# Attention tail sums spread one to every three steps, and a reordered start of the first unit

## Chip, core and metric

The kernel runs on one core of a Trainium2 chip. Its engines are PE (TensorE, matrix products and transposes), ACT (ScalarE), DVE (VectorE), POOL (GpSimd) and SP, whose queue issues the DMAs. Each engine runs its own instructions strictly in the order in which the program holds them, and waits for semaphores of the others. The metric is the device time of one execution in microseconds (us); lower is better.

## What is computed

The reference is three blocks in a row on a sequence of 1024 tokens and width 1024: a hybrid layer (stick-breaking attention and two gated linear recurrences), a block of an RWKV time mix beside a dilated window attention, and a block of spatial gating and Fourier mixing. The change touches two places: the very first projection, and the dilated attention, for each of 16 heads of width 64:

```python
DILATED_PATTERNS = ((128, 1), (512, 4), (2048, 16))

def mixed_dilated_attention(p_att, gate):
    q, k, v = (t.reshape(B, S, ATT_HEADS, HEAD_DIM) for t in jnp.split(p_att, 3, axis=-1))
    for window, dilation in DILATED_PATTERNS:
        o, lse = dilated_window_attention(q, k, v, window, dilation)   # softmax inside a window
        ...
    wts = jax.nn.softmax(jnp.stack(lses, axis=0), axis=0)
    o = jnp.sum(wts[..., None] * jnp.stack(outs, axis=0), axis=0)
    return o.reshape(B, S, ATT_W) * jax.nn.silu(gate)
```

## The kernel before

**The first unit.** A "unit" is one 128-column slice of a projection: its weights W (128 x 1024 f32) are loaded, split by ACT into a rounded part (`w_hi`) and by DVE into the rest (`w_lo`), and PE multiplies with the input, which is split in the same way into `xs` (`x_hi` on ACT, `x_lo` on DVE), in eight slices k. Each of the two halves of 512 tokens takes 8 x 3 matmuls of 128x512 (`mm3`), so a unit is 48 matmuls. At the start SP issues the eight slices of the input first, and then the weights of the first two units (`b1_sp`). ACT and DVE split all eight slices and do five tiny operations on gate constants (`lbl`, with one exponential `lb_exp` on ACT) before the split of the first weights (`b1_act`, `b1_dve`). `unit_pe` does half 0 through all eight slices and then half 1. After four units the stick-breaking attention begins (`sb_act`, `sb_dve`).

**The dilated attention** runs over eight pairs of heads, p = 0 to 7. What each engine does for a pair is written as generators that yield at each step, and `weave` takes one step of each in turn, which fixes the order of an engine's instructions: in a stage p the main part of pair p (39 steps), the tail of pair p-1, and the three projection units of pair p+1 (8 steps each, so they fill steps 0 to 23). Steps are counted from 0 here.

- Main (`att_pe_main`, `att_act_main`, `att_dve_main`): ten pieces. In step 3i PE makes the scores of piece i, DVE adds the mask and takes the minimum (`a_max`), ACT takes the exponential (`a_exp`); in step 3i+1 PE turns (transposes) the exponentials of piece i-2 (`a_t`, two PSUM banks, one for each head) and DVE copies them out (`PT`); in step 3i+2 PE multiplies piece i-3 with the values (`a_av`), and ACT copies finished outputs (`a_osc`).
- Tail: POOL spreads the minima (x = 0) and the sums (x = 1) of the softmax over a tile `XM`, six copies each; PE turns each with four transposes (`spread_pe`, `xm_t`). ACT copies those of x = 0 to `MB`, DVE forms the common minimum and the differences (`mb_min`, `mb_sub`), ACT their exponentials (`mb_e`), DVE weights and adds the three outputs (`o_w`, `o_add`), multiplies by the gate (`gated_o`), multiplies the turned sums of x = 1 into `MB` (`den`), adds them (`den_sum`), takes the reciprocal in four pieces and multiplies it in (`att_out`), which SP stores.
- The turned exponentials and the turned `XM` take the same two PSUM banks in turn (ring `RT`). An `a_t` that falls on the bank of an `xm_t` of x = 1 waits for its `den`.
- The third unit of a stage is the gate. Its eviction on ACT (a silu, line L301, in steps 21 and 23) writes the buffer that `gated_o` of the pair two before reads, which is the pair whose tail runs in the same stage; so it waits for that `gated_o` (`att_units_act`).

After the last pair its tail runs alone; then follows the next part of the kernel, whose constants are loaded after the store of the last `att_out`.

## Time and profile before

| | us |
|---|---|
| median of 3 runs | 3436.62 |
| lowest and highest | 3430.69, 3438.08 |
| the profiled execution | 3428.97 |
| its span | 3427.6 |
| the six attention stages with a tail and units | 82.1 to 84.1 each |

The profiled execution is one run; the views below are all read from it. Each stage of the attention is measured from the start of one pair's first scores (or its last transposes) to the same point of the next.

### The profile page before, as it was taken

The page shows a single profiled execution, that of the slowest core. Times are in us where ns is not written, and L with a number is a line of the kernel's source. Part 1 is how long each engine was busy: PE and PEld are TensorE (multiplying, and loading weights), DVE is VectorE, ACT ScalarE, POOL GpSimd, SP SyncE. Part 2 cuts the span into 40 slices and gives each one's busy share as a digit, 9 for nine tenths or more (in the row PEclk, how much of TensorE's full clock was granted, in tenths as well). Part 3 has the DMA queues.
Part 4 walks back from the last instruction along what each step waited for, and adds up shares of the span by engine and source line. Part 5 has one row for each costly group of instructions (what it writes and reads, how often), then busy time and mean ns, then how long its engine had stood idle before and what let it go on. Part 6 is the DMA issues. An engine that isn't in the chain of part 4 may idle for free. (4 is left out here: it accounts for less than half of the span.)

```text
span 3427.6 us, 66797 instructions
## 1 busy us (share of the span) xinstructions
PE 3070.9 (90%) x28304; PEld 2464.4 (72%) x28304; DVE 1946.3 (57%) x3481; ACT 1326.7 (39%) x2364; POOL 127.4 (4%) x132
## 2 busy tenths in 40 slices
PE   7988999999989988888867999969898889999998
PEld 5665777866767766666645787859787887777876
DVE  3555566523474367677764545646666666545465
ACT  3344343221244455555551444422222223453224
POOL 0000000000000112112210000000000000000000
PEclk9998999999999999999988999979999999999999
DMA  3000011242245311111101233341112115341114
GB/s 109 19 19 19 31 39 55 62 165 70 75 133 166 94 40 48 44 45 49 44 32 50 80 129 129 117 189 50 50 55 73 47 56 210 123 140 62 37 46 157
DMA packets 106089, 270.73 MB, mean 79 GB/s; under 512 B 8880, under 2 KB 49472, under 8 KB 104256
## 3 DMA queue, kind: packets, MB, share of 16 engines
q1 hardware_dynamic: 105792, 266.47, 23.3%
q8 instruction: 224, 3.67, 0.5%
q14 instruction: 73, 0.60, 0.1%
HBM read 209.81 MB, written 56.62 MB: 78 GB/s over the span
## 5 line engine op out<-in xcount | busy, mean ns | idle before, releaser
L197 PE MATMUL ps<-xs,wparts 128*128 128x512 f32 (+1 forms) x1664 | 697.2, 419 | 29.2 <-DVE wparts L265 28.3
L199 PE MATMUL ps<-xs,wparts 128*128 128x512 f32 (+1 forms) x1664 | 656.5, 395 | 0.0
L198 PE MATMUL ps<-xs,wparts 128*128 128x512 f32 (+1 forms) x1664 | 655.8, 394 | 0.0
L265 DVE TENSOR_TENSOR wparts<-wring,wparts 128x1024 fp32r<-128x1024 f32 x248 | 305.8, 1233 | 327.4 <-ACT wparts L257 301.5
L197 PEld LDWEIGHTS ps<-xs,wparts 128*128 128x128 f32 (+1 forms) x1664 | 315.5, 190 | 131.5 <-issue 59.9
L257 ACT ACTIVATE wparts<-wring 128x1024 fp32r<-128x1024 f32 x248 | 262.8, 1060 | 299.2 <-PE ps L199 210.8
L199 PEld LDWEIGHTS ps<-xs,wparts 128*128 128x128 f32 (+1 forms) x1664 | 314.5, 189 | 71.9 <-issue 0.6
L198 PEld LDWEIGHTS ps<-xs,wparts 128*128 128x128 f32 (+1 forms) x1664 | 316.0, 190 | 60.8 <-issue 4.6
L2066 ACT ACTIVATE Pm<-Pm,ml 128x128 f32<-128x128 f32 (+1 forms) x384 | 167.4, 438 | 178.0 <-DVE ml L2131 177.8
L2131 DVE CUSTOM_DVE_ANT_0 Pm<-ps,mask 128x128 f32<-128x128 f32 (+1 forms) x384 | 110.4, 347 | 139.0 <-PE ps L1974 139.0
L2427 ACT ACTIVATE M<-ps 128x256 f32<-128x256 f32 x160 | 61.5, 384 | 255.7 <-PE ps L2238 246.9
L2523 DVE COPY_PREDICATED XX<-lm,ps 128x512 f32<-128x512 uint8 (+1 forms) x160 | 107.9, 674 | 79.8 <-PE ps L2238 76.7
L2238 PE MATMUL ps<-XX,M 64*64 64x64 f32 x2560 | 144.4, 219 | 5.7 <-issue 3.1
L1987 PE MATMUL ps<-cc,Pm 128*128 128x128 f32 x560 | 83.6, 289 | 67.1 <-DVE MB L2179 50.1
L197 PE MATMUL ps<-wparts,mixA 128*128 128x512 f32 x320 | 129.0, 403 | 12.2 <-DVE wparts L265 9.4
L2238 PEld LDWEIGHTS ps<-XX,M 64*64 64x64 f32 x2560 | 128.9, 135 | 9.3 <-issue 6.5
L2238 PE MATMUL ps<-M,XX 64*64 64x64 f32 x2048 | 124.9, 218 | 2.5 <-issue 2.5
L1987 PEld LDWEIGHTS ps<-cc,Pm 128*128 128x128 f32 x560 | 66.4, 147 | 83.2 <-DVE MB L2179 52.7
L199 PE MATMUL ps<-wparts,mixA 128*128 128x512 f32 x320 | 126.0, 394 | 0.0
L198 PE MATMUL ps<-wparts,mixA 128*128 128x512 f32 x320 | 125.7, 393 | 0.0
L197 PE MATMUL ps<-wparts,xs 128*128 128x512 f32 x256 | 105.0, 410 | 13.7 <-DVE wparts L265 13.7
L2238 PEld LDWEIGHTS ps<-M,XX 64*64 64x64 f32 x2048 | 112.3, 135 | 2.3 <-issue 2.2
(400 smaller groups left out, 5823.8 us busy)
## 6 DMA issues: line engine op xcount, KB each, us to landing
wring<-in_wo SPq DMA_DIRECT2D x96, 512.0 KB, 3.7
ops<-rw SPq DMA_DIRECT2D x32, 640.0 KB, 6.0
wring<-in_w SPq DMA_DIRECT2D x39, 512.0 KB, 3.7
wring<-in_w2u SPq DMA_DIRECT2D x33, 512.0 KB, 3.9
wring<-in_wg SPq DMA_DIRECT2D x24, 512.0 KB, 3.6
wring<-in_w2v SPq DMA_DIRECT2D x24, 512.0 KB, 4.1
wring<-in_w2a SPq DMA_DIRECT2D x24, 512.0 KB, 4.5
Vc<-vr SPq DMA_DIRECT2D x32, 256.0 KB, 3.4
```

Source lines behind the costliest of these rows:

```text
L197: nc.tensor.matmul(out, a, c, start=start, stop=False)
L198: nc.tensor.matmul(out, b, c, start=False, stop=False)
L199: return nc.tensor.matmul(out, a, d, start=False, stop=stop)
L257: K.nc.scalar.activation(W.part(i, 0), W.raw(i), ACT.Copy).then_inc(*K.act.done("w_hi", W.first + i))
L265: K.nc.vector.tensor_tensor(W.part(i, 1), W.raw(i), W.part(i, 0).bitcast(F32), ALU.subtract).then_inc(*K.dve.done("w_lo", W.first + i))
L1987: a = nc.tensor.transpose(bank[:, half(x, 128)], B.Pm[:, (NS * p + n) % 3, h, b[0]:b[0] + 128], K.ident)
L2066: a = nc.scalar.activation(P, P, ACT.Exp, scale=-1.0, bias=ml[:, 0, s.pi, h, c:c + 1], accum_out=ml[:, 1, s.pi, h, c:c + 1])
L2131: a = nc.vector.tensor_tensor_reduce(B.Pm[:, (NS * p + i) % 3, h, lo:hi], K.bank["a_s", p, i, h][:, lo:hi], m, 1.0, 3e38, ALU.add, ALU.min ...
L2238: a = nc.tensor.matmul(out[rr], lhs[rr], rhs[rr], start=start, stop=stop, skip_group_check=True)
L2427: nc.scalar.activation(dst.rearrange("p c x -> p (c x)"), bank[:, 0:256], ACT.Copy).then_inc(*act.done(*done))
L2523: nc.vector.copy_predicated(XX[:, 0:kinds], B.lm64[:, l, 0:kinds, :].unsqueeze(2).to_broadcast([128, kinds, 4, 64]), K.bank["xt_mm", s, n, ...
```

## The change

1. **Start.** SP loads the first weights ahead of the eight input slices, and the second weights directly after them. ACT and DVE split the first weights first. The gate constants (`lbl`, `lb_exp`) and the cast of the mask `lm` come only after the first four units. The first unit has its own function, which takes both halves of each slice k before the next slice.
2. **Attention, PE.** `paced` puts two more empty steps behind every step of a generator. The six turned sums of x = 1 come in steps 12, 15, 18, 21, 24 and 27, not in steps 12 to 17.
3. **Attention, DVE.** The tail does one operation in most steps: the two minima and three differences in steps 6 to 10, then for each of the three patterns the weighting, one `den`, the addition, the other `den` and the sum, in steps 11 to 28, the reciprocals in 29 to 32 and `att_out` in 33 (it was in 22). `gated_o` moves from step 12 to step 26. Each `den` now also waits for DVE's own operation before it. The weighting waits for its own exponential, not for all three.
4. **Attention, ACT.** The three exponentials come two steps later; the rest is empty steps.

```diff
+def paced(gen, n, m):
+    x, at = next(gen), 0
+    while True:
+        if x is STEP:
+            at += m - n
+            yield STEP
+            while at >= n:
+                at -= n
+                yield STEP
+        try:
+            x = next(gen) if x is STEP else gen.send((yield x))
+        except StopIteration:
+            return
...
+    yield from w_load(K, B.W, 0)
     for i in range(8):
         nc.sync.dma_start(B.T[:, i, :], A["xT"][:, i, :]).then_inc(*sp.done("x_load", i, slot=i, by=16))
+    yield from w_load(K, B.W, 1)
     nc.sync.dma_start(B.cols[:, :], A["c1"]).then_inc(*sp.done("c1", by=16))
-    for i in range(2):
-        yield from w_load(K, B.W, i)
...
+def first_unit_pe(K, W, i, xs, xkeys, ring, free):
+    nc, n = K.nc, W.first + i
+    banks = [ring.take(("u", n, h), (free, n, h))[0] for h in range(2)]
+    K.pe.wait_ge(*(yield "w_lo", n))
+    wh, wl = columns(W.part(i, 0)), columns(W.part(i, 1))
+    for k in range(8):
+        K.pe.wait_ge(*(yield xkeys[k]))
+        for h, bank in enumerate(banks):
+            a = mm3(nc, bank, (wh[:, k, :], wl[:, k, :]), (xs[:, 0, k, half(h)], xs[:, 1, k, half(h)]), k == 0, k == 7)
+            if k == 7:
+                a.then_inc(*K.pe.done("u", n, h))
+        if k < 7:
+            yield STEP
...
 def b1_act(K, A, B):
+    yield from w_hi(K, B.W, 0)
     (x_hi of the eight slices)
+    yield from weave(sb_units_act(K, B, 0))
     act.wait_ge(*(yield "lbl", 0))
     act.in_order()
     nc.scalar.activation(B.z1, B.z1, ACT.Exp).then_inc(*act.done("lb_exp"))
-    yield from w_hi(K, B.W, 0)
-    yield from weave(sb_units_act(K, B, 0))
...
@@ att_pe_tail
-    yield from spread_pe(K, B, p, 1)
-    for _ in range(5):
+    yield from paced(spread_pe(K, B, p, 1), 1, 3)
+    for _ in range(4):
         yield STEP
...
@@ att_dve_tail
     for pi in range(3):
-        dve.wait_ge(*(yield "mb_e", p, 2))
-        dve.wait_ge(*(yield "a_osc", p, 2, 1))
+        dve.wait_ge(*(yield "mb_e", p, pi))
+        dve.wait_ge(*(yield "a_osc", p, pi, 1))
         dve.in_order()
         nc.vector.tensor_tensor(O[:, pi, :], O[:, pi, :], MB[:, pi, :], ALU.mult).then_inc(*dve.done("o_w", p, pi))
-        dve.in_order()
+        yield STEP
+        yield from den_dve(K, B, p, pi, 0)
+        yield STEP
         if pi:
+            dve.in_order()
             nc.vector.tensor_tensor(O[:, 0, :], O[:, 0, :], O[:, pi, :], ALU.add).then_inc(*dve.done("o_add", p, pi))
+        yield STEP
+        if pi == 2:
+            dve.wait_ge(*(yield "uev", ATT_W0 + 3 * p + 2, 1))
             dve.in_order()
-        yield STEP
-    dve.wait_ge(*(yield "uev", ATT_W0 + 3 * p + 2, 1))
-    nc.vector.tensor_tensor(O[:, 0, :], O[:, 0, :], B.qkg[:, p % 2, 2, :], ALU.mult).then_inc(*dve.done("gated_o", p))
...
+            nc.vector.tensor_tensor(O[:, 0, :], O[:, 0, :], B.qkg[:, p % 2, 2, :], ALU.mult).then_inc(
+                *dve.done("gated_o", p))
+        yield STEP
+        yield from den_dve(K, B, p, pi, 1)
+        yield STEP
+        if pi:
+            dve.in_order()
+            nc.vector.tensor_tensor(den, MB[:, 0, :] if pi == 1 else den, MB[:, pi, :], ALU.add).then_inc(
+                *dve.done("den_sum", p, pi))
+        yield STEP
```

**In the programs' order.** The first instructions of ACT, before and after (`xs<-xT` is `x_hi`, `wparts<-wring` is `w_hi`, `cols<-cols` is `lb_exp`, `h<-ps` the first eviction):

```order
L1075 ACTIVATE xs<-xT 128x1024 [waits x_hi,x_or_up_2]
L1078 ACTIVATE cols_8<-cols_8 128x2 [waits x_hi,b1_setup]
L257 ACTIVATE wparts<-wring 128x1024 [waits b1_norm_act,w_load20]
L257 ACTIVATE wparts<-wring 128x1024 [waits w_hi,w_load21]
L301 ACTIVATE h<-ps 128x512 [waits w_hi,u,x_lo]
```

```order
L273 ACT_TABLE_LOAD [waits barrier_Pool_Activation_PE_DVE_SP_release]
L273 ACTIVATE wparts<-wring 128x1024 [waits w_load20]
L1108 ACTIVATE xs<-xT 128x1024 [waits w_hi,x_or_gate_0]
L1108 ACTIVATE xs<-xT 128x1024 [waits x_hi,x_or_gate_1]
L1108 ACTIVATE xs<-xT 128x1024 [waits x_hi,x_or_gate_2]
```

The split of the first weights has moved from behind all eight input slices and `lb_exp` to the front.

DVE in one stage of the attention, steps 9 to 13 before (the two rows of `Pm` stand four times each in the program between `wparts` and `O<-O,qkg`; the first pair is shown):

```order
L2167 TENSOR_TENSOR O<-O,MB 128x1024
L2143 COPY PT<-ps 128x512 x2
L2167 TENSOR_TENSOR O<-O,MB 128x1024
L2170 TENSOR_TENSOR O<-O 128x1024
L2167 TENSOR_TENSOR O<-O,MB 128x1024
L2170 TENSOR_TENSOR O<-O 128x1024
L265 TENSOR_TENSOR wparts<-wring,wparts 128x1024
L2131 ISA Pm,ml<-ps,mask 128x128
L2131 ISA ml 128x1
L2174 TENSOR_TENSOR O<-O,qkg 128x1024
L2179 TENSOR_TENSOR MB<-ps,MB 128x512
L2143 COPY PT<-ps 128x512 x2
```

DVE in the same stage now, the end of it, steps 27 to 34 (the last `a_max` row of piece 9, then the tail and the copies of pieces 7, 8 and 9):

```order
L2165 ISA Pm,ml<-ps,mask 128x128
L2165 ISA ml 128x1
L2238 TENSOR_TENSOR MB<-ps,MB 128x8x64
L2177 COPY PT<-ps 128x384 x2
L2221 TENSOR_TENSOR den<-den,MB 128x1024
L2226 RECIPROCAL den<-den 128x256 x2
L2177 COPY PT<-ps 128x512 x2
L2226 RECIPROCAL den<-den 128x256 x2
L2229 TENSOR_TENSOR O<-O,den 128x1024
L2177 COPY PT<-ps 128x512 x2
```

The first `den` no longer has five operations of the outputs ahead of it; the last `den`, the sum, four reciprocals and `att_out` have moved in among the copies of the last three pieces, where before only the copies stood.

ACT at the gate's eviction, now (before, the same rows stood in the same places):

```order
L317 ACT_TABLE_LOAD [waits a_exp,u]
L317 ACTIVATE qkg<-ps 128x512 [waits a_tail]
L317 ACTIVATE qkg<-ps 128x512 [waits uev,u]
L2098 ACT_TABLE_LOAD
L2098 ACTIVATE Pm,ml<-Pm,ml 128x128 [waits a_max]
L2098 ACTIVATE Pm,ml<-Pm,ml 128x128 x3
```

Nothing moved here on ACT, but the semaphore `a_tail` that the second row waits for is now raised by DVE in step 26 and not in step 12; behind it in ACT's order stand the exponentials of pieces 8 and 9.

## Rows read from the trace of the kernel before

**Rows 1.** The page: busy us, share of the span, instructions.
```profile
PE 3070.9 (90%) x28304; PEld 2464.4 (72%) x28304; DVE 1946.3 (57%) x3481; ACT 1326.7 (39%) x2364; POOL 127.4 (4%) x132
```

**Rows 2.** Timeline of the start: start us, us, engine, line, operation, [idle before <-releaser].
```profile
5.58 1.06 ACT L1075 ACTIVATE xs<-xT 128x1024 fp32r<-128x1024 f32 x1 [3.56 <-DMA xT<-in_xT]
...
6.67 10.53 DVE L1386 TENSOR_TENSOR xs<-xT,xs 128x1024 fp32r<-128x1024 f32 x8 [5.80 <-ACT xs L1075]
6.86 1.06 ACT L1075 ACTIVATE xs<-xT 128x1024 fp32r<-128x1024 f32 x1 [0.22 <-DMA xT<-in_xT]
...
18.95 1.23 DVE L265 TENSOR_TENSOR wparts<-wring,wparts 128x1024 fp32r<-128x1024 f32 x1 [0.45 <-ACT wparts L257]
...
20.28 0.77 PE L197 MATMUL ps<-xs,wparts 128*128 128x512 f32 x1 [20.28 <-DVE wparts L265]
...
25.11 0.47 PE L199 MATMUL ps<-xs,wparts 128*128 128x512 f32 x1
```

**Rows 3.** Timelines of ACT and PE in the stick-breaking attention.
```profile
68.50 1.28 ACT L956 ACT_TABLE_LOAD   x1
...
148.09 1.55 PE L687 MATMUL ps<-h 64*128 64x512 f32 x4 [1.04 <-ACT h L959]
```

**Rows 4.** Windows by stage of the attention: us, busy of PE, PEld, DVE, ACT, POOL, clock, DMA.
```profile
1301.40:1383.50 82.10, 70.60 (x499) 53.51 (x499) 58.27 (x143) 44.83 (x122) 15.62 (x17) 0.96 0.14 46
...
1714.80:1789.00 74.20, 46.44 (x355) 34.99 (x356) 54.25 (x140) 35.70 (x112) 7.78 (x13) 0.77 0.11 36
```

**Rows 5.** What PE waited for, 1157 to 1850: us in total, times, longest.
```profile
PE ps L1987 <- DVE MB L2179: 50.1, 8, 7.0
...
PE ps L1987 <- DVE PT L2143: 10.2, 9, 3.2
```

**Rows 6.** Timeline of PE around the long wait of one stage.
```profile
1342.72 1.12 PE L1987 MATMUL ps<-cc,Pm 128*128 128x128 f32 x4 [6.99 <-DVE MB L2179]
...
1345.35 0.63 PE L199 MATMUL ps<-xs,wparts 128*128 128x512 f32 x1
...
1354.99 0.63 PE L2017 MATMUL ps<-cc,XM 128*128 128x128 f32 x4 [1.30 <-DVE PT L2143]
```

**Rows 7.** Timeline of DVE in that stage.
```profile
1358.66 1.09 DVE L2179 TENSOR_TENSOR MB<-ps,MB 128x512 f32<-128x512 f32 x1 [1.92 <-PE ps L2017]
...
1378.26 0.29 DVE L2131 CUSTOM_DVE_ANT_0 Pm<-ps,mask 128x128 f32<-128x128 f32 x1 [0.41 <-PE ps L1974]
...
1379.96 1.02 DVE L2143 COPY PT<-ps 128x384 f32<-128x384 f32 x2
1381.39 1.29 DVE L2143 COPY PT<-ps 128x512 f32<-128x512 f32 x2 [0.42 <-PE ps L1987]
```

**Rows 8.** Timeline of PE at the end of that stage.
```profile
1373.93 1.16 PE L1974 MATMUL ps<-perm 64*128 64x128 f32 x16
...
1377.06 1.16 PE L1974 MATMUL ps<-perm 64*128 64x128 f32 x16 [0.36 <-DVE ml L2131]
...
1383.49 1.09 PE L1987 MATMUL ps<-cc,Pm 128*128 128x128 f32 x8 [0.96 <-ACT Pm L2066]
```

**Rows 9.** Timeline of ACT at the end of that stage.
```profile
1376.11 0.40 ACT L2066 ACTIVATE Pm<-Pm,ml 128x128 f32<-128x128 f32 x1
...
1379.39 1.11 ACT L2078 ACTIVATE O<-ps 128x512 f32<-128x512 f32 x1
```

**Rows 10.** Timeline of PE in the last stage, which has no units.
```profile
1722.77 0.63 PE L2017 MATMUL ps<-cc,XM 128*128 128x128 f32 x4 [2.47 <-ACT MB L2092]
...
1728.70 1.08 PE L2017 MATMUL ps<-cc,XM 128*128 128x128 f32 x4 [3.14 <-ACT MB L2092]
```

**Rows 11.** Timeline of the last tail: DVE, and SP's store.
```profile
1807.17 2.48 DVE L2167 TENSOR_TENSOR O<-O,MB 128x1024 f32<-128x1024 f32 x2 [1.18 <-ACT MB L2098]
...
1823.10 7.12 DVE L2188 RECIPROCAL den<-den 128x256 f32<-128x256 f32 x4
...
1831.50 0.33 SPq L1904 DMA_DIRECT2D mix<-O  x1
```

More of the change, by code:

```diff
@@ L641, in sb_units_pe @@
     for u in range(4 * p, 4 * p + 4):
-        yield from unit_pe(K, B.W, u, B.xs, B.xkeys, B.units, "uev")
+        yield from (unit_pe if u else first_unit_pe)(K, B.W, u, B.xs, B.xkeys, B.units, "uev")
         yield STEP
@@ L1382, in b1_dve @@
     nc.vector.memset(B.one[:, :], 1.0).then_inc(*dve.done("one"))
+    yield from w_lo(K, B.W, 0)
     for i in range(8):
@@ L1387, in b1_dve @@
             *dve.done("x_lo", i))
+    yield from weave(sb_units_dve(K, B, 0))
     z1, lb = B.z1, B.lb
@@ L1401, in b1_dve @@
     dve.in_order()
-    yield from w_lo(K, B.W, 0)
     dve.wait_ge(*(yield "lm_load", 0))
@@ L1407, in b1_dve @@
     dve.wait_ge(*(yield "tri"))
-    yield from weave(sb_units_dve(K, B, 0))
     yield from weave(sb_dve(K, B, 0), sb_units_dve(K, B, 1))
@@ L2099, in att_act_tail @@
         yield STEP
-    for _ in range(3 + 6 + 5):
+    for _ in range(23):
         yield STEP
@@ L2163, in att_dve_tail @@
     for pi in range(3):
-        dve.wait_ge(*(yield "mb_e", p, 2))
-        dve.wait_ge(*(yield "a_osc", p, 2, 1))
+        dve.wait_ge(*(yield "mb_e", p, pi))
+        dve.wait_ge(*(yield "a_osc", p, pi, 1))
         dve.in_order()
         nc.vector.tensor_tensor(O[:, pi, :], O[:, pi, :], MB[:, pi, :], ALU.mult).then_inc(*dve.done("o_w", p, pi))
-        dve.in_order()
+        yield STEP
+        yield from den_dve(K, B, p, pi, 0)
+        yield STEP
         if pi:
+            dve.in_order()
             nc.vector.tensor_tensor(O[:, 0, :], O[:, 0, :], O[:, pi, :], ALU.add).then_inc(*dve.done("o_add", p, pi))
+        yield STEP
+        if pi == 2:
+            dve.wait_ge(*(yield "uev", ATT_W0 + 3 * p + 2, 1))
             dve.in_order()
+            nc.vector.tensor_tensor(O[:, 0, :], O[:, 0, :], B.qkg[:, p % 2, 2, :], ALU.mult).then_inc(
+                *dve.done("gated_o", p))
         yield STEP
-    dve.wait_ge(*(yield "uev", ATT_W0 + 3 * p + 2, 1))
-    nc.vector.tensor_tensor(O[:, 0, :], O[:, 0, :], B.qkg[:, p % 2, 2, :], ALU.mult).then_inc(*dve.done("gated_o", p))
-    for pi in range(3):
-        for gg in range(2):
-            m, r = group(MB[:, pi, :], pi, gg)
-            dve.wait_ge(*(yield "xm_t", p, 1, pi, gg))
-            nc.vector.tensor_tensor(m, runs(K.bank["xm_t", p, 1, pi, gg], r), m, ALU.mult).then_inc(
-                *dve.done("den", p, pi, gg))
-            if pi and gg:
-                dve.in_order()
-                nc.vector.tensor_tensor(den, MB[:, 0, :] if pi == 1 else den, MB[:, pi, :], ALU.add).then_inc(
-                    *dve.done("den_sum", p, pi))
-            yield STEP
+        yield from den_dve(K, B, p, pi, 1)
+        yield STEP
+        if pi:
+            dve.in_order()
+            nc.vector.tensor_tensor(den, MB[:, 0, :] if pi == 1 else den, MB[:, pi, :], ALU.add).then_inc(
+                *dve.done("den_sum", p, pi))
+        yield STEP
     for x in range(4):
@@ L2192, in att_dve_tail, with den_dve @@
     yield STEP
+def den_dve(K, B, p, pi, gg):
+    m, r = group(B.MB[:, pi, :], pi, gg)
+    K.dve.wait_ge(*(yield "xm_t", p, 1, pi, gg))
+    K.dve.in_order()
+    K.nc.vector.tensor_tensor(m, runs(K.bank["xm_t", p, 1, pi, gg], r), m, ALU.mult).then_inc(
+        *K.dve.done("den", p, pi, gg))
 def att_dve(K, A, B):
```

## Prediction, made before the changed kernel ran

> **What bounds the kernel now.** I read the page first: PE is busy for 90% of the span and DVE for 57% [rows 1], so only what keeps PE waiting, or starts it late, can be gained. The change touches two places where it does.
>
> The first is the start. PE's first matmul waits until 20.28 us, for DVE's split of the first weights, which ends 0.1 us earlier [rows 2]. From then on it runs at 1.2 GHz for 4.8 us (to 25.11), and at 2.4 GHz afterwards.
>
> The second is the attention. A stage with units takes 82.1 us, of which PE is busy for 70.6, DVE for 58.3 and ACT for 44.8 [rows 4]. The list of PE's waits puts 50.1 us in 8 waits on `den` (L2179) [rows 5]: one of 7 us in each stage with a tail. The timeline shows it between the two heads' turned exponentials of piece 2 (6.99 us), the half clock behind it (0.63 us a matmul at 1345.35), and a wait of 1.30 us for a copy later on [rows 6]. At that time DVE has its five operations of the outputs ahead of the `den`. The same timeline shows PE short of work at the end of the stage, where no unit stands between the pieces: waits of 0.36 and 0.96 us [rows 8]. There DVE and ACT have little but the pieces to do. That is where the change puts DVE's work.
>
> **The start.** The terms are read from the profiled execution (3428.97 us: its span of 3427.6 and 1.4 around it). The median of the runs is 7.7 us above it, so the sum of the terms is added to the median. The first 512 KB arrive for ACT's start at 5.58, the next 1.28 us later (6.86) [rows 2]. The weights now take the first place: `w_hi` 5.58 to 6.64, `w_lo` (1.23) to 7.9. The first slice is one place later: `x_hi` 6.86 to 7.92, `x_lo` to 9.25. So PE starts at 9.3 instead of 20.28. DVE delivers a slice every 1.32 us (10.53 for eight), and with both halves side by side PE needs 6 matmuls a slice: 2.6 us at the half clock (0.43 from start to start), 1.4 at the full one. PE is never ahead of DVE, and the last slice, due at 18.5, is needed later. The second weights arrive at 16.9, are split by 19.8, and unit 0 ends near 22.5. The gain is 20.3 - 9.3 = **11.0 us**; 10 to 11.5 with the moment at which the clock rises.
>
> Moved for it are the gate constants and the cast of `lm`. Behind the fourth unit ACT now loads the exponential's table (1.28 us, as at 68.50), takes 0.2 us, and loads a table again, and DVE does six short operations: 1.5 to 1.9 us before the first sigmoid. PE first waits for these engines at 148.09 [rows 3]; until then unit matmuls cover it. I take 0, and 1.9 as the other end. The Trainium skill (ScalarE: Activation LUTs, section What ACT_TABLE_LOAD costs) counts about 2.66 us for a switch, because a drain comes on top of the 1.28; the row shows only the 1.28. By the page the delay would be 2.9 and the sum would still be the same, as long as PE's cover holds.
>
> **The attention, up to step 24.** Gone are 6.99 + 1.30 us of waiting and about half of the 3.7 us that PE then runs at 1.2 GHz (1342.72 to 1346.4) [rows 6]: 10.2 us a stage. The `den` of x = 1 now come one to three steps, with two unit groups between them, so up to step 21 I find waits of a few tenths only. Step 24 (scores of piece 8) began 69.3 us after the stage's start (1373.93 less 1304.6) [rows 8]; now at 59.1.
>
> **From step 24 on.** Units are over in step 23, and every turning of the second head now waits for the `den` before it, which stands on DVE behind an `a_max`, which waits for PE's scores. I lay DVE's new order out with the measured times [rows 7, 8]: scores of piece 8 with the hand-over 1.2; `a_max` 1.7 (1378.26 to 1379.96); `den` 1.09; PE's turning 0.35; copies 1.02; addition and gate 2 x 1.24 [rows 11]; `a_max` of piece 9 1.7; `den` 1.09; turning 0.35; copies 1.02; sum 1.24; four reciprocals 7.12 [rows 11]; copies of piece 8 1.29; `att_out` 1.24; copies of piece 9 1.29; PE's last product 1.0. That is 25.2 us: the stage ends at 59.1 + 25.2 = 84.3, against 82.1. So the 10.2 us are given back, and **2.2 us** more, in each of six stages: +13.2.
>
> The added wait on ACT: the gate's eviction (step 21) now waits for `gated_o` (step 26), and behind it are queued the exponentials of pieces 8 and 9, for which PE waits. It costs ACT about 10 us of standing still. `gated_o` ends at 59.1 + 7.8 = 66.9; evictions 1.3, table 1.3, exponentials 3.2 (1376.11 to 1379.3), output copy 1.1, exponentials 3.2 [rows 9], turning 1.1 [rows 8] make 78.1. DVE gets to the copies of piece 9 only at 82.0, so this chain is second by 4 us and adds nothing; if DVE were faster, it would be the bound, 82.1 - 78.1 less copies and product (2.3) = 1.7 us below today's stage. That is the lower end, with DVE's hand-overs hidden: -1.7. The upper end is a PE at half clock through the end of the stage and the first steps of the next: the last product and turnings twice as long, 1.3, and half of some 4 us of units as behind today's stall, 2: +5.5. The middle, 2.2, is the plain sum, nearest to the rows.
>
> SP: the store of `att_out` comes 10 us later, but the loads queued behind it wait for the products of pieces 7 and 9 anyway, and the last is later than `att_out`: 0. POOL's copies follow PE, and its next permutations wait for scores of steps 21 and 27 as before: 0.
>
> **The last stage and its tail.** The last stage (74.2 us) has no units, so its stall of 7 goes while DVE's 54.3 us of work stay [rows 4]; I take -1. In the last tail the weighting no longer waits for the third exponential, 1.18 us [rows 11], and all of it ends in the store on which the next part hangs; the ordered `den` cost a few tenths. Together **-2**, from 0 to -5.
>
> **Sum.** -11.0 + 13.2 - 2 = +0.2 us: 3436.62 becomes **3437**. A difference under 0.2% (6.9 us) is about what a measurement of this kernel can't tell from none.
>
> **Rivals.**
> (a) *The end of the stage holds DVE's work.* Where hand-overs overlap and ACT's chain decides, a stage is between -1.7 and +1.0. For it: DVE has 24 us idle in a stage. Against it: most of these lie in steps 0 to 5, before the tail's first DVE work, where the change doesn't use them. At 0 a stage the time is 3436.6 - 11 - 2 = 3424. Below +1.0 a stage the kernel is faster by over 6.9 us. Chance 0.3.
> (b) *The half clock.* PE's wait before the second head of piece 7 comes out at 3.5 to 3.8 us (scores 9, then `a_max` and `den` on DVE). In the last stage, where PE is as sparse, a wait of 2.47 us left the clock at 2.4 GHz (0.63 for four turnings) and one of 3.14 was followed by 1.2 GHz (1.08) [rows 10], and the granted clock of that stage was 0.77 against 0.96 [rows 4]. If it falls in every stage and stays low until the next stage's units, a stage costs +4.5: 27 - 2 - 11 = +14, 3451. It decides from +3.3 a stage. The Trainium skill (TensorE: Matmul & The Clock Gate, section A second HAM failure mode: psum-queue depth-cycling) says that short idle spells between groups, as the banks are cycled, make the clock go back and forth; the row of the last stage agrees. Chance 0.2.
> (c) *The start gives nothing*, because the weights arrive late or a later wait takes it back: +11, 3448. Chance 0.05; the arrivals are in the rows.
> (d) The forecast, within 6.9 us: 0.45.
>
> **Numbers.** Faster 0.30 (a), same 0.45, slower 0.25 (b, c). The range runs from 3421, (a) with the tail's best, to 3451, (b).
>
> **What would show it.** PE's first matmul near 9.3, unit 0's end near 22.5. The 7 us wait on `den` gone; instead, in every stage, PE waits for `den` of 2 us before piece 6 and 3.5 before piece 7, for an exponential before piece 8, and for the copies before the last product. ACT idle some 10 us before the third unit's eviction, put down to `gated_o`. Stages of 84.3 us: under 82 speaks for (a), over 86 with a granted clock under 0.9 for (b). I am wrong if PE's waits from step 24 on sum to less than 6 us, or if the start comes later than 11 us.

## The result, and the profile after

| | before | after |
|---|---|---|
| median, us (5 runs each) | 3435.18 | 3451.09 |
| lowest and highest | 3430.69, 3438.08 | 3446.75, 3453.45 |
| span of the profiled execution | 3427.6 | 3448.0 |

The ratio is 1.0046, with a 95% interval of 1.0032 to 1.0061: 0.46% slower, where 3437 us and no measurable change were forecast. The time lies at the upper edge of the range (3451), 14 us above the forecast itself. The other kernels below were timed on other occasions, each time with the kernel before beside them, whose median was then 3432.0, 3433.2 or 3431.0 us; so ratios are compared below, and not the medians alone.

PE's busy time grew, although it does the same work [rows 1]. The page of the kernel after:

```profile
PE 3107.2 (90%) x28304; PEld 2488.6 (72%) x28304; DVE 1957.0 (57%) x3481; ACT 1328.0 (39%) x2365; POOL 129.1 (4%) x132
```

The start, PE and DVE (start, duration, engine, line, operation, idle before and who ended it), to be held against [rows 2]:

```profile
9.70 0.76 PE L213 MATMUL ps<-xs,wparts 128*128 128x512 f32 x1 [9.70 <-DVE xs L1419]
...
15.37 0.40 PE L214 MATMUL ps<-xs,wparts 128*128 128x512 f32 x1
```

```profile
7.00 1.23 DVE L281 TENSOR_TENSOR wparts<-wring,wparts 128x1024 fp32r<-128x1024 f32 x1 [6.13 <-ACT wparts L273]
8.33 10.53 DVE L1419 TENSOR_TENSOR xs<-xT,xs 128x1024 fp32r<-128x1024 f32 x8
```

What PE waited for in the attention (1140 to 1850: us in total, times, longest), against [rows 5]:

```profile
PE ps L2019 <- DVE MB L2238: 47.3, 36, 3.6
PE ps L2032 <- DVE PT L2177: 20.8, 7, 4.4
```

The 8 waits of up to 7 us on a `den` have become 36 of at most 3.6, with nearly the same total, and the wait on the copies before the last product, 0.4 us in total in the kernel before, is now 20.8 in seven waits. The end of one stage on PE, without the unit matmuls, against [rows 8] (L2006 scores, L2019 turned exponentials, L2032 product with the values, L2049 a turned sum):

```profile
1362.62 1.16 PE L2006 MATMUL ps<-perm 64*128 64x128 f32 x16
...
1366.78 0.71 PE L2019 MATMUL ps<-cc,Pm 128*128 128x128 f32 x3 [2.08 <-DVE MB L2238]
1367.42 1.55 PE L2032 MATMUL ps<-PT,Vc 128*64 128x128 f32 x12
1368.90 1.88 PE L2006 MATMUL ps<-perm 64*128 64x128 f32 x16
...
1373.79 0.88 PE L2019 MATMUL ps<-cc,Pm 128*128 128x128 f32 x3 [2.10 <-DVE MB L2238]
...
1376.55 1.97 PE L2019 MATMUL ps<-cc,Pm 128*128 128x128 f32 x8 [0.40 <-ACT Pm L2098]
...
1380.79 1.94 PE L2019 MATMUL ps<-cc,Pm 128*128 128x128 f32 x8 [0.79 <-DVE PT L2177]
...
1387.42 1.93 PE L2032 MATMUL ps<-PT,Vc 128*64 128x128 f32 x16 [2.99 <-DVE PT L2177]
1389.28 1.65 PE L2006 MATMUL ps<-qkg 64*128 64x128 f32 x8
```

Eight transposes take 1.97 us here, where they took 1.09 before [rows 8]: PE did them at 1.2 GHz. The windows say the same (us, busy of PE, PEld, DVE, ACT, POOL, granted clock): 0.72 over the end of the stage, with DVE busy for 24.3 of 30 us.

```profile
1333.00:1361.00 28.00, 27.07 (x188) 19.83 (x186) 17.84 (x46) 12.20 (x38) 5.94 (x6) 1.00 0.07 19
1361.00:1391.00 30.00, 21.64 (x153) 16.74 (x152) 24.28 (x53) 12.90 (x39) 5.06 (x5) 0.72 0.12 37
...
1367.10:1370.40 3.30, 3.30 (x29) 2.65 (x28) 2.81 (x4) 0.00 (x0) 0.00 (x0) 0.50 0.00 0
1370.50:1373.80 3.30, 1.20 (x14) 0.84 (x10) 3.05 (x19) 2.97 (x6) 2.95 (x2) 1.00 0.01 5
1373.90:1384.00 10.10, 8.90 (x56) 7.14 (x58) 9.41 (x9) 7.75 (x32) 1.94 (x3) 0.50 0.00 0
1384.20:1387.40 3.20, 0.23 (x6) 0.01 (x1) 3.04 (x4) 1.05 (x1) 0.00 (x0) 1.00 0.15 63
```

The shorter windows show that the clock was not down throughout. It went back and forth, and the two stretches at 2.4 GHz were stretches in which PE mostly waited (busy for 1.20 of 3.30 us and for 0.23 of 3.20), so they gave little back.

This stage stands for three of the six (the second, fourth and sixth). In the other three the wait of 2.08 us left the clock up, and it fell only with a longer wait before the second head of piece 7 (3.2 to 3.6 us). The first of them:

```profile
1279.84 0.55 PE L2019 MATMUL ps<-cc,Pm 128*128 128x128 f32 x3 [2.08 <-DVE MB L2238]
...
1286.44 0.90 PE L2019 MATMUL ps<-cc,Pm 128*128 128x128 f32 x3 [3.24 <-DVE MB L2238]
```

DVE at the end of the stage shown first, its last ten microseconds:

```profile
1376.56 3.54 DVE L2226 RECIPROCAL den<-den 128x256 f32<-128x256 f32 x2
1380.02 1.22 DVE L2177 COPY PT<-ps 128x512 f32<-128x512 f32 x2
1381.27 3.54 DVE L2226 RECIPROCAL den<-den 128x256 f32<-128x256 f32 x2
1384.85 1.23 DVE L2229 TENSOR_TENSOR O<-O,den 128x1024 f32<-128x1024 f32 x1
1385.99 1.28 DVE L2177 COPY PT<-ps 128x512 f32<-128x512 f32 x2
```

The copies for which PE's last product waits stand behind the reciprocals and `att_out`.

**Where the time went.** The table is worked out from the starts of DVE's first `a_max` of each pair and each piece. "Attention at" is the first of all. "To piece 8", "late part" (from piece 8 to the next stage) and "stage" are means over the six stages with a tail and units. The last columns are the stage without units, up to its last copies, and the rest up to the last `att_out`. All times in us; the rows below those of before and after are the experiments. All but the median is read from one profiled execution each. An `a_max` can start well after the scores that it reads, when DVE has other work first, so a difference of some tenths between two columns need not be PE's.

| kernel | attention at | to piece 8 | late part | stage | last stage | last tail | median |
|---|---|---|---|---|---|---|---|
| before | 1158.0 | 70.1 | 12.6 | 82.7 | 71.6 | 40.6 | 3435.2 |
| after | 1151.7 | 60.1 | 26.7 | 86.8 | 70.8 | 41.8 | 3451.1 |
| start_only | 1149.8 | 70.0 | 12.6 | 82.6 | 71.6 | 40.5 | 3424.8 |
| start_const | 1154.7 | 70.4 | 12.6 | 83.0 | 72.2 | 40.6 | 3423.9 |
| att_only | 1159.7 | 60.3 | 26.7 | 87.1 | 70.8 | 41.6 | 3459.1 |
| third_gate | 1151.2 | 60.4 | 27.2 | 87.6 | 72.7 | 41.7 | 3453.1 |
| no_recip | 1149.0 | 61.4 | 22.5 | 83.9 | 65.7 | 33.1 | 3411.3 |
| gate_recip | 1151.4 | 61.5 | 19.2 | 80.6 | 63.1 | 33.1 | 3394.7 |
| fill | 1146.8 | 60.9 | 27.5 | 88.3 | 72.7 | 41.7 | 3457.3 |
| fill_small | 1148.5 | 60.5 | 24.9 | 85.4 | 70.7 | 41.7 | 3442.3 |
| early_tail | 1152.2 | 65.4 | 16.4 | 81.7 | 70.3 | 40.8 | 3418.2 |
| dve_order | 1152.1 | 67.5 | 12.7 | 80.2 | 72.1 | 40.9 | 3410.9 |
| plan_a | 1150.9 | 62.3 | 12.6 | 74.9 | 68.5 | 40.3 | 3375.2 |
| plan_b | 1149.8 | 60.9 | 12.6 | 73.5 | 68.0 | 40.2 | 3364.9 |

Between the two profiled executions: the attention starts 6.3 us earlier, six stages cost 4.15 us more each (24.9), the last stage and tail 0.4 more, and what follows the attention 1.6 more: 20.6 against a span 20.4 longer. The last term is scatter: over the other kernels, all alike there, it lies between 0 and 5.8 us above before.

### The profile page after: what moved, and what is told of

Read it like the earlier page. It is cut to its first block and busy times, and to the rows that moved or that the text cites. A ratio compares the mean times of both kernels' runs of the same rounds, so it can differ in the third digit from the quotient of the medians.

```text
span 3448.0 us, 66868 instructions
## 1 busy us (share of the span) xinstructions
PE 3107.2 (90%) x28304; PEld 2488.6 (72%) x28304; DVE 1957.0 (57%) x3481; ACT 1328.0 (39%) x2365; POOL 129.1 (4%) x132
## 5 line engine op out<-in xcount | busy, mean ns | idle before, releaser
L2019 PE MATMUL ps<-cc,Pm 128*128 128x128 f32 x560 | 97.0, 311 | 61.3 <-DVE MB L2238 47.3
L2019 PEld LDWEIGHTS ps<-cc,Pm 128*128 128x128 f32 x560 | 74.0, 158 | 82.5 <-DVE MB L2238 56.1
L2032 PE MATMUL ps<-PT,Vc 128*64 128x128 f32 x1120 | 99.2, 328 | 20.9 <-DVE PT L2177 20.8
```

Source lines behind the costliest of these rows:

```text
L2019: a = nc.tensor.transpose(bank[:, half(x, 128)], B.Pm[:, (NS * p + n) % 3, h, b[0]:b[0] + 128], K.ident)
L2032: a = nc.tensor.matmul(ob[rr, half(c % 4, 128)], B.Vc[:, 8 * s.pi + kc, rr], B.PT[:, (NS * p + n) % 2, h, half(x, 128)], start=new, stop=e ...
```

## Experiments

### The two parts apart

`start_only` is before with part 1 of the change, `att_only` before with parts 2 to 4.

> The kernel before with the change at the start alone; the attention is as before. In the changed kernel's profile the first unit ends 10.4 us earlier, but the first scores of the attention start only 6.3 us earlier than before. Theory A (some of the gain is lost between the start and the attention, whatever the attention does): the attention starts about 6 us earlier, its stages stay at 82 us, and the time falls by 6 us, from 3435 to 3429. Rival (what is lost is scatter between two profiled executions): the time falls by the full 10.5 us, to 3425.

> The kernel before with the change in the attention alone; the start is as before. Theory (the two parts are independent, and the attention alone costs what the stages of the changed kernel show): six stages of 86.8 us in place of 82.6, 25 us in all, so 3435 becomes 3460. Rival (an interaction: the later start of the change shifts the phase of the stages and so the granted clock): stages of 84 us, 3444.

Measured: 0.9981 (0.9970 to 0.9992) and 1.0078 (1.0063 to 1.0093) of before, that is -6.5 and +26.8 us; their sum, +20 with 4 to 5 us of uncertainty on each, agrees with the +15.9 of both together. The parts are independent: stages of 82.6 us with the one and 87.1 with the other. The start gives less than the 10.3 us by which unit 0 ended earlier in the kernel after, whatever the attention is; the interval of `start_only`, -2.7 to -10.3 us, only just leaves out the full gain.

The lost part shows where the stick-breaking attention begins. PE's waits from 9 to 75 us in `start_only`:

```profile
PE ps L213 <- DVE xs L1419: 9.6, 1, 9.6
PE ps L730 <- DVE h L1250: 1.7, 1, 1.7
```

The second is new. ACT in the kernel after, at that place:

```profile
58.24 1.28 ACT L1112 ACT_TABLE_LOAD   x1
59.53 0.21 ACT L1112 ACTIVATE cols<-cols 128x2 f32<-128x2 f32 x1
59.81 1.28 ACT L988 ACT_TABLE_LOAD   x1
61.11 0.28 ACT L988 ACTIVATE h<-ps 128x128 f32<-128x128 f32 x1
```

These are the moved `lb_exp` and its table loads; the first sigmoid stands behind them, DVE's chain on it behind that, and PE's first product with `h` behind that. In the kernel before, the same chain had no slack either: PE made the product 0.06 us after DVE's last operation on `h`.

```profile
71.65 0.29 DVE L1218 TENSOR_TENSOR h<-h,pr 128x128 f32<-128x128 f32 x1
```

```profile
72.00 0.33 PE L698 MATMUL ps<-cc,h 128*128 128x128 f32 x1
```

`start_const` puts the constants ahead of the four units (the edit is against `start_only`):

```diff
@@ b1_act
+    act.wait_ge(*(yield "lbl", 0))
+    act.in_order()
+    nc.scalar.activation(B.z1, B.z1, ACT.Exp).then_inc(*act.done("lb_exp"))
     yield from weave(sb_units_act(K, B, 0))
-    act.wait_ge(*(yield "lbl", 0))
-    act.in_order()
-    nc.scalar.activation(B.z1, B.z1, ACT.Exp).then_inc(*act.done("lb_exp"))
@@ b1_dve
-    yield from weave(sb_units_dve(K, B, 0))
     z1, lb = B.z1, B.lb
...
+    yield from weave(sb_units_dve(K, B, 0))
     dve.wait_ge(*(yield "lm_load", 0))
```

> The change at the start alone, but with the gate constants (lb_exp on ACT, five short operations on DVE) behind the split input and ahead of the four units. Theory (of the 10.5 us that the first unit gains, 1.5 to 2 are lost by the second table load, 1.28 us, and the constants themselves, at 60 to 70 us): the attention starts 2 us earlier than in the run with the start alone, 3425 becomes 3423. Rival (the delay there is covered by PE's units and the rest is scatter): no difference.

Measured: 3423.94 us, 0.9971 (0.9960 to 0.9981). The wait of 1.7 us is gone from its trace, and the first table load of the exponential with it:

```profile
58.28 1.28 ACT L988 ACT_TABLE_LOAD   x1
59.58 0.28 ACT L988 ACTIVATE h<-ps 128x128 f32<-128x128 f32 x1
```

Of the time, no difference can be told from `start_only`. The split of the third, fourth and fifth weights (ACT) comes 10.7 to 10.8 us earlier than before in the mean of the eleven other kernels with the change at the start, that of the sixth (70.47 before) only 9.2. In `start_const` all four come 10.2 us earlier: nothing is lost where the others lose 1.6. Some 70 us later the executions scatter by 1 us, at the attention by 1.8: the 1 us gained can't be followed to the end.

### Is it ACT's stand before the gate, or DVE's chain?

`third_gate` gives the gates three buffers, so that the eviction waits for the `gated_o` of the pair before. `no_recip` leaves out the four reciprocals (the outputs are multiplied by the sums). `gate_recip` does both.

```diff
@@ third_gate
-    B.qkg, B.PT = sb("qkg", [128, 2, 3, 1024]), sb("PT", [128, 2, 2, 512])
+    B.gates, B.qkg, B.PT = sb("gates", [128, 3, 1024], mybir.dt.bfloat16), sb("qkg", [128, 2, 2, 1024]), sb("PT", [128, 2, 2, 512])
...
-        old = [] if p < 2 else [("gated_o", p - 2)] if i == 2 else [("a_s", p - 2, LAST[0]), ("perm", p - 2, 2)]
+        old = ([("gated_o", p - 3)] if p >= 3 else []) if i == 2 else [] if p < 2 else [("a_s", p - 2, LAST[0]), ("perm", p - 2, 2)]
...
@@ no_recip
     for x in range(4):
-        dve.in_order()
-        nc.vector.reciprocal(den[:, half(x, 256)], den[:, half(x, 256)]).then_inc(*dve.done("den_inv", p, x))
         yield STEP
```

> The changed kernel with three buffers for the gates in place of two, held in bf16 so that they fit; the gate's eviction on ACT then waits for the gated_o of the pair before, and stands still no longer. Theory A (the end of a stage is held by DVE's chain, in which two of the four reciprocals stand ahead of the copies of piece 8): ACT's idle time of 10.9 us before the third unit's eviction goes, PE's wait of 0.40 us for the exponentials of piece 8 goes, and a stage gets shorter by 0 to 0.5 us: 3451 becomes 3448 to 3451. Rival B (ACT's chain of eviction, table, exponentials and copies holds it): a stage falls by 4 us, and the time to 3427.

> The changed kernel without the four reciprocals of each tail (7.1 us of DVE in a stage); the outputs are multiplied by the sums and not divided by them. Theory A (DVE's chain holds the end of a stage, ACT's is second): DVE is free at 1376.6 where it was at 1387, and what is late then is the exponentials of piece 9 on ACT (end 1380.43), their turning and their copies; the last product starts at 1383.2 and not at 1387.4: 4.2 us a stage, 25 us for six, and 7 us of the last tail, 3451 becomes 3419. Rival C (the end of a stage is long because PE runs at the half clock, DVE's work is beside it): stages stay within 1 us of 86.8, only the last tail's 7 us go, 3444.

> Both edits together: three gate buffers in bf16, and no reciprocals (the outputs are multiplied by the sums, not divided). With the reciprocals in place the third buffer moved nothing. Theory A (ACT's chain behind gated_o is second in line, and is the bound once the reciprocals are gone): PE's waits for the exponentials of pieces 8 and 9, 0.59 and 0.66 us in the run without reciprocals, go, and a stage gets 1 to 2 us shorter than there, 3411 becomes 3402. Rival (ACT's stand of 11 us never matters): the same 3411.

Measured: `third_gate` 1.0061 (1.0043 to 1.0079), like the kernel after. The type bf16 of the gates is not what hides a gain: the eviction (0.60 us) and `gated_o` (1.23 us) take as long as before. In after ACT stands still six times:

```profile
ACT qkg L317 <- DVE O L2214: 64.9, 6, 11.1
```

Taking that stand away gives nothing, as the prediction said. The exponentials come earlier, but PE then waits for DVE's copies, 2.45 us before piece 9 is turned where it was 0.79:

```profile
1383.15 1.94 PE L2019 MATMUL ps<-cc,Pm 128*128 128x128 f32 x8 [2.45 <-DVE PT L2177]
```

`no_recip` is at 0.9933 (0.9912 to 0.9954), some 40 us below the kernel after. Its late part is 4.2 us shorter, just what was expected of the end of a stage. The stage as a whole is only 2.9 shorter (83.9), because the part up to piece 8 takes 1.3 more: ACT waits longer for the load of the stage's first weights (19.3 us in six stages, 12.3 in after), and PE behind it for the turned minima (11.6 us, 4.2 in after). The total fell by more than was expected all the same: I had counted the last tail's reciprocals, and forgotten that those of the tail inside the last stage have no cover either (70.8 to 65.7). What is late in its stages is ACT:

```profile
1371.31 1.97 PE L2019 MATMUL ps<-cc,Pm 128*128 128x128 f32 x8 [0.59 <-ACT Pm L2098]
...
1375.42 1.09 PE L2019 MATMUL ps<-cc,Pm 128*128 128x128 f32 x8 [0.66 <-ACT Pm L2098]
```

`gate_recip` takes that away too: 0.9891 (0.9875 to 0.9907), a late part of 19.2, 3.3 below `no_recip` where 1 to 2 were expected. So DVE's chain bounds the end of the stage, and ACT's is second by about 4 us.

### What does the half clock cost?

`fill` and `fill_small` keep PE busy in its waits at the end of a stage with products that nobody reads, 12, 12 and 20 or 6, 6 and 8 of them (the profile lists each as two instructions).

```diff
@@ fill_small against after, att_pe_main, turned exponentials
             for h, (bank, old) in enumerate(banks):
+                if h and 0 < p < 7 and i in (8, 9):
+                    yield from fill_pe(K, B, 6)
@@ products with the values
+            if 0 < p < 7 and n == 9:
+                yield from fill_pe(K, B, 8)
```

> The changed kernel with products of a constant, whose results nobody reads, put where PE waits late in stages 1 to 6: 12 of 128x128 before the second head of pieces 6 and 7 is turned, 20 before the last product. They write a bank of scores that is overwritten next, and wait for the a_max that frees it. Theory B (the wait of 2.1 us is what drops the granted clock, and the lower clock costs about 2 us at the end of each stage: the last product 1.93 in place of 1.09, the turnings of pieces 8 and 9 1.95 in place of 1.04, of which half is hidden behind the reciprocals): the clock of the end of a stage rises from 0.72 to over 0.9, a stage goes from 86.8 to 85, and 3451 becomes 3440. Rival A (PE's clock there is covered by DVE's work): the clock rises, stages stay within 0.5 us, and the time stays at 3451.

> The changed kernel with fewer products of a constant in PE's waits at the end of a stage: 6 before the second head of pieces 6 and 7, 8 before the last product. With 12 and 20 of them the granted clock of the stage rose to 0.99, but the 20 took 4.73 us at a place where the wait was 3.0, and the last product started 1.7 us after the copies it needs. Theory A (PE's clock at the end of a stage is covered by DVE's work): the late part (piece 8 to the next stage) stays at 26.7 us less the last product's 0.8, so a stage is 86, and the time 3447. Theory B (the half clock costs 2 us or more): a stage is 84.8 or less, 3439.

Measured: `fill` 1.0071 (1.0058 to 1.0084). Taken alone it would speak for theory A: the granted clock is 1.00 and 0.98 over two of its stages and the time no better. But its products were too many, as its trace shows (the copies for the last product end at 1383.4):

```profile
1380.44 4.73 PE L1994 MATMUL ps<-cc 128*128 128x128 f32 x40
1385.10 1.09 PE L2043 MATMUL ps<-PT,Vc 128*64 128x128 f32 x16
```

It hides its gain behind a loss of its own and decides nothing. `fill_small` is at 1.0036 (1.0024 to 1.0049). By the ratios that is only 3 us below the kernel after, with some 6 of uncertainty; the span is 8.3 us shorter. The timed runs don't settle it, the stages in the trace do. The window over the late part of a stage (in after, over the late part of the stage above, the granted clock is 0.69), and PE's first wait there:

```profile
1358.80:1383.70 24.90, 18.38 (x169) 15.05 (x170) 21.91 (x51) 12.82 (x39) 6.08 (x4) 0.93 0.11 32
```

```profile
1359.79 1.60 PE L1994 MATMUL ps<-cc 128*128 128x128 f32 x12
1361.82 0.55 PE L2028 MATMUL ps<-cc,Pm 128*128 128x128 f32 x3 [0.42 <-DVE MB L2249]
```

Its late part is 24.9 us (24.8 to 25.2 in the six stages), that of the kernel after 26.7 (26.2 to 27.2). Its stage of 85.4 lies between the two theories' numbers. With the clock held up, the end of a stage takes what the plain sum of the prediction said (25.2). The half clock costs 1.8 us of the late part, and DVE's chain the other 12.3 of the 14.1 that the late part grew. DVE's run from the last `den_sum` to the last copy is 12.0 us long in both kernels (1375.30 to 1387.27 in after); what got shorter is PE's work ahead of it and the last product behind it, 1.09 us and not 1.97. Of the whole stage, 1.4 us are gained (86.8 to 85.4). The other 0.4 is lost again up to piece 8, where ACT waits longer for the load of the weights, as in `no_recip` (15.6 us in six stages).

### Other orders of the tail

If DVE's work was only put in the wrong place, other orders should give both gains. `dve_order` leaves PE and ACT as before (with the start of the change) and gives DVE each `den` in its own step; `early_tail` keeps the change's idea, with the turned sums in steps 12, 13, 15, 16, 18 and 19:

```diff
@@ early_tail, att_pe_tail
-    yield from paced(spread_pe(K, B, p, 1), 1, 3)
+    yield from paced(spread_pe(K, B, p, 1), 2, 3)
@@ dve_order against before, att_dve_tail, steps 12 to 14 (early_tail likewise, with its own steps)
-    for pi in range(3):
-        for gg in range(2):
...
+    yield from den_dve(K, B, p, 0, 0)
+    yield STEP
+    yield from den_dve(K, B, p, 0, 1)
+    yield STEP
+    yield from den_dve(K, B, p, 1, 0)
+    add(1)
+    yield STEP
```

DVE's operations by step, in order (w weighting, d `den`, a addition, S sum, g `gated_o`, r reciprocal, o `att_out`):

```
dve_order   9 w0 | 10 w1 | 11 w2 | 12 d00 | 13 d01 | 14 d10 a1 | 15 d11 | 16 d20 S1 | 17 d21 | 18 a2 g | 19 S2 | 20 to 23 r | 24 o
early_tail  11 w0 | 12 d00 | 13 d01 w1 | 14 a1 | 15 d10 | 16 d11 | 17 S1 w2 | 18 d20 | 19 d21 | 20 S2 a2 g | 21 to 24 r | 25 o
```

> The change at the start, and in the attention PE's and ACT's order as before (the six turned sums in steps 12 to 17): only DVE's order is changed, each den directly in its step, one addition or sum behind it, the three weightings in steps 9 to 11, gated_o in 18, the reciprocals in 20 to 23. Theory A (the stall of before came from the five operations ahead of the den, not from PE's six turnings in a row): the wait of 7 us falls below 2, a stage is 76 to 78 us, and the time is 3435 - 8 - 6 x 5 = 3397. Rival (six turnings in six steps are too dense for DVE, so spreading them was needed): stages of 81 or more, 3420.

> The changed kernel with the six turned sums in steps 12, 13, 15, 16, 18 and 19 in place of 12 to 27, the last sum, addition and gated_o in step 20, the reciprocals in steps 21 to 24. Theory A (DVE's work was moved to where PE has no units to cover it; moved back beside the units, with each den directly behind its transposes, both the stall of before and the long end go): piece 8 starts about 61 to 63 us after the stage's start, the end of the stage takes 13 to 15 us as before, a stage is 75 to 77 us, and the time is 3435 - 8 - 6 x 6.5 = 3388. Rival (DVE has too much to do in steps 12 to 23, and PE waits for it there as before): stages of 82, 3427.

Measured: `dve_order` 0.9933 (0.9921 to 0.9945), `early_tail` 0.9952 (0.9940 to 0.9965). Both beat both kernels, and both fall short of what was expected: the stages of `dve_order` (80.2) lie between its theory and its rival, those of `early_tail` (81.7) at its rival's 82. `dve_order` still has a wait on the first `den`, up to 3.7 us where below 2 was expected; on DVE two weightings and the split of a unit's weights stand directly ahead of it:

```profile
PE ps L2019 <- DVE MB L2251: 26.3, 8, 3.7
```

`early_tail` loses its gain from step 20 on. DVE and POOL there:

```profile
1352.32 1.23 DVE L2211 TENSOR_TENSOR den<-den,MB 128x1024 f32<-128x1024 f32 x1
1353.58 1.23 DVE L2207 TENSOR_TENSOR O<-O 128x1024 f32<-128x1024 f32 x1
1354.91 3.06 DVE L2238 TENSOR_TENSOR O<-O,qkg 128x1024 f32<-128x1024 f32 x1
...
1359.12 1.75 DVE L2242 RECIPROCAL den<-den 128x256 f32<-128x256 f32 x1
```

```profile
1354.84 5.06 POOL L1949 COPY perm<-qkg 128x1024 f32<-128x1024 f32 x2 [12.90 <-PE ps L2006]
```

The `gated_o` takes 3.06 us instead of 1.23: POOL's permutation started 0.07 us before it (the section on the hardware has more such cases). That is 1.8 us. The late part is 3.8 us longer than before, and how the rest divides between the full step 20 and the clock, which is granted at 0.61 to 0.80 in its late parts, no run here separates.

`plan_a` and `plan_b` take both lessons:

```diff
@@ att_pe_tail (the second argument: empty steps ahead of each turned sum)
-    for _ in range(6):
-        yield STEP
-    yield from paced(spread_pe(K, B, p, 1), 1, 3)
+    yield from spaced(spread_pe(K, B, p, 1), (5, 1, 0, 0, 1, 0))
@@ plan_a, DVE's operations by step (m minimum, s difference, t sum)
+TAIL_DVE = {6: "m0 m1", 7: "s0", 8: "s1 s2", 9: "w0", 10: "w1", 11: "d00", 13: "w2 d01 a1", 14:
+            "d10", 15: "d11 a2", 17: "g t1 d20", 18: "d21 t2", 20: "r0 r1", 22: "r2", 23: "r3", 24:
+            "o"}
@@ plan_b, where it differs (and ACT's exponentials in steps 6, 7 and 11, not 7, 8 and 9)
+TAIL_DVE = {5: "m0 m1", 6: "s2", 8: "s0 s1",
```

> The change at the start, and a third order for the tail: the turned sums in steps 11, 13, 14, 15, 17 and 18, the minima in 6, differences in 7 and 8, weightings 0 and 1 in steps 9 and 10 and 2 in 13, each den in its step, additions in 13 and 15, gated_o in 17, the last sum in 18, reciprocals in 20 (two), 22 and 23, att_out in 24. Theory A (two things decide: that nothing long stands on DVE between the transposes of a sum and the turning two steps later, and that no operation of DVE with two SBUF inputs falls on POOL's permutations in steps 21 to 24, where gated_o took 3.06 us in place of 1.23 in the run before): the waits on den fall below 1 us, the end of the stage takes 12 to 13 us, a stage is 74 to 76 us, and the time is 3435 - 8 - 6 x 7.5 = 3382. Rival (DVE is too full in steps 9 to 24 whatever the order): stages of 80 us as with the order of the run before, 3411.

> As the run before, but the two minima in step 5, the third difference before the other two, and the third exponential four steps later on ACT. Theory A: the same as the run before within 1 us a stage, 3376 to 3388; the order of these does not matter as long as each den stands free. Rival (the earlier minima make DVE wait for ACT's last copy of step 5): stages 2 us longer, 3394.

Measured: `plan_a` 0.9836 (0.9821 to 0.9851), as expected; `plan_b` 0.9807 (0.9790 to 0.9824), 10 us better than `plan_a` where none was expected. By PE's scores the two kernels take the same 6.07 us from piece 2 to piece 3. The difference comes after it: to piece 4 it is 9.30 us in `plan_a` and 8.16 in `plan_b`, because PE waits for DVE's copies in between. The same place of one stage, in `plan_a` and in `plan_b`:

```profile
1318.65 0.63 PE L2044 MATMUL ps<-cc,XM 128*128 128x128 f32 x4 [1.56 <-DVE PT L2169]
...
1314.23 0.63 PE L2044 MATMUL ps<-cc,XM 128*128 128x128 f32 x4 [0.44 <-DVE PT L2170]
```

In `plan_a` DVE is still behind there: both minima stand after the `a_max` of piece 2 and the three differences after them, and its `a_max` of piece 3 starts 3.8 us after PE began the scores (1311.29 to 1315.08), against 2.7 in `plan_b` (1308.02 to 1310.67), where the minima come first. I had not looked at this. Three things were changed together (the minima, the order of the differences, the third exponential), and no run separates them. `plan_b` is the best kernel of this study, 1.9% below before. One of its stages as a window, against [rows 4]:

```profile
1289.00:1363.00 74.00, 69.31 (x501) 52.20 (x500) 58.35 (x146) 45.08 (x123) 17.45 (x17) 1.00 0.16 51
```

DVE does the same 58 us of work as in a stage before, in 74 us instead of 82, and the granted clock is 1.00.

## Where the prediction held and where it failed, point by point

The time is within the range, the mechanisms that the forecast named are in the trace, and still the forecast itself (3437, no change) missed. Its three terms erred in the same direction, so that nothing cancelled. The step that failed is the price of the late part: it was worked out for a PE at the full clock.

- **The start, -11.0.** PE's first matmul came at 9.70 (predicted 9.3), the full clock at 15.37, and the last matmul of unit 0 began at 23.12 (33.38 before), so that the unit ended 1.0 us later than the 22.5 forecast. The next units' weights were split 10.2 us earlier in this execution and 10.8 in the mean of the eleven kernels with the same start. This step is right to 0.2 us in the mean, and inside its 10 to 11.5 in each.
- **The moved constants, 0.** Wrong, with 1.6 us. I looked at PE's first long wait [rows 3] and called all before it covered. But a chain that ends just in time leaves no wait in the list and has no slack: DVE's `h` ended 0.06 us before PE used it. The range's other end (1.9) was the better value. The start's gain at the attention was 8.5 us (the mean of eleven kernels against the mean of before and `att_only`), where 11.0 were forecast; 1.6 of the missing 2.5 us are this step, the other 0.9 has no cause that a run shows.
- **Up to step 24, -10.2 a stage.** Measured -10.0 by the table (70.1 to 60.1), and -9.4 counted from PE's scores, as the prediction counts (69.8 to 60.4). Right to within a few tenths.
- **The late part, 25.2 us.** The failed step is the choice of the middle, 2.2 a stage, "the plain sum, nearest to the rows": it took PE's clock as full. At the full clock the sum is right (24.9 in `fill_small`, 25.1 from PE's scores); in fact the late part took 26.7 (26.3 from PE's scores), and a stage cost 4.15 us more than before. That is within the bounds (-1.7 to +5.5) and near the 4.5 of rival (b), whose mechanism it is. (b) is not right in full: the clock did not stay down, it went back and forth; it fell after 2.08 us of waiting in three stages and after 3.2 to 3.6 in the others. I had the rows for it: [rows 10] show a wait of 2.47 that left the clock up and one of 3.14 that did not, in a stage with a granted clock of 0.77 [rows 4], and I had worked out waits of 2 and 3.5 us in each stage. The two together, in a stretch without units, resembled that stage and not the one with units. Rival (b) deserved more than 0.2.
- **The waits.** Before the second head of piece 6 2.08 us in every stage (about 2 predicted). Of piece 7 3.2 to 3.6 where the clock was still up (3.5 to 3.8 predicted), and 2.1 where it had fallen: there PE was itself late, with 1.88 us for the scores of piece 9, not 1.16. In the stage shown, before the exponentials of piece 8 0.40, before the last product 2.99. All four signs were there, and the waits sum to 8.4 us, above the 6 below which the prediction would have been wrong. ACT stood 10.9 us (10 predicted), and stages of 86.8 us are the sign that was named for (b), with a granted clock of 0.89 in three of them (0.91 to 0.93 in the others, where under 0.9 was named).
- **ACT's chain second by 4 us, adds nothing.** Right: `third_gate` and `gate_recip`.
- **Last stage and tail, -2.** Measured +0.4. The stage gained 0.8 (-1 forecast). The tail lost 1.2 instead of gaining 1: 1.3 more before its first minimum, where PE turns the first minima at 1.2 GHz, and from the first minimum to `att_out` 32.0 us as before (32.2): the 1.18 us that no longer waits for the third exponential went into the ordered `den` between.
- **The sum.** -8.5 + 24.9 + 0.4 = +16.8, against +15.9 measured. Of the 16.6 us between this and the forecast's +0.2, 11.7 come from the stages, 2.5 from the start, 2.4 from the tail. Of the 11.7, 8.4 (1.4 in each of six stages) are the half clock by `fill_small`; the rest is spread over the stage and has no term of its own.
- **The range.** Its upper end, 3451, is right by luck as far as the last microseconds go: (b) put 27 us on the stages, 2.1 too many, and 4.9 too few on start and tail. The range was also narrower than its own terms: -1.7 to +5.5 a stage alone gives 3413 to 3457.

## What to carry to other kernels

A stall is not removed by moving the work that makes it to where the waiting engine has nothing to cover it: the change freed 10.0 us a stage and paid 14.1. Before work is spread over steps, note in which of them the covering work ends, and end the spread there: the units end in step 23, and the best kernel has its last turned sum in step 18 and `att_out` in 24, where the change had them in 27 and 33. The same operations in another order gave 9.2 us a stage instead of costing 4.2. And where new waits come into a stretch in which TensorE is already sparse (here of 2.1 and 2.1 to 3.6 us), price the stretch at the half clock too: the clock fell in all six. A chain that leaves no wait in the list may still have no slack.

## What the runs showed of the hardware

A DVE operation with two inputs in SBUF that started while POOL copied from SBUF waited for that copy to end. Over the traces of all fourteen kernels, 53 operations of 128x1024 started during a permutation copy (2.0 us); all took 1.70 to 3.07 us, and each ended 1.08 to 1.10 us after the end of the copy. The 1527 others in the attention took 1.24 in the mean and 1.57 at most. The 48 reciprocals, with one input, that started in a copy took 1.75 like the other 336. POOL is held up as well: the two copies of `early_tail` above took 5.06 us together, where 2 x 2.0 is usual. The Trainium skill (SBUF — State Buffer, section SBUF: two separate sides) says that the pair of ports that the two engines share is locked for the whole instruction, by whichever starts first; the traces agree. The price was up to 1.83 us an operation. In the kernel after, six sums fell on a copy in step 22, as this row shows; in this stage DVE then had to wait for PE's scores anyway (0.31 us idle), so it cost nothing:

```profile
1359.53 2.63 DVE L2221 TENSOR_TENSOR den<-MB 128x1024 f32<-128x1024 f32 x1
```

The granted clock fell after a wait of 2.08 us in a stage whose stretch before had 27.07 of 28 us of PE busy, and in the stage before that one the same wait of 2.08 us left it up. In [rows 10] a wait of 2.47 us did not lower it. The length of the one wait does not separate the cases, and no run here shows what does. It also came back without dense work: it was at 1.00 from 1370.5 to 1373.8 and from 1384.2 to 1387.4, with PE busy for 1.20 and 0.23 us of these.
